# Hybrid encoder layer on one core: all operands of TensorE moved to one start address modulo 256 bytes in SBUF

## The chip, the cores and the metric

The kernel runs on one core of one Trainium2 chip. The metric is the device time of one execution in microseconds. A core has five engines that run side by side: TensorE (PE in the profile: matmuls; PEld: its weight loads, which run beside the matmuls), VectorE (DVE), ScalarE (ACT), GpSimd (POOL) and SyncE (SP, which issues the DMAs). All of them work on SBUF, 128 partitions of a fixed number of bytes each. A tensor in SBUF has a byte address that is the same in every partition; this case is about that address.

## The reference

One layer of a hybrid encoder on 1024 tokens of width 1024, with 16 meta tokens put before them, so 1040 positions, all in float32:

```python
hn = rms_norm(h, g_mix_pre)
proj = hn @ w_in          # c_q 384, c_kv 256, k_rope 64, and seven parts of 1024
a = mla(c_q, c_kv, k_rope, ...)      # 8 heads of attention, softmax over 1040 keys
r = hgrn2(hq, hf_fwd, hf_bwd, hi, hg, lb, g_norm)   # 8 heads, a gated recurrence in both directions
mixed = sigmoid(gate_a) * a + sigmoid(gate_h) * r
h = h + rms_norm(mixed @ w_o, g_mix_post)
hn = rms_norm(h, g_ffn_pre)
ff = (silu(hn @ w_gate) * (hn @ w_up)) @ w_down     # inner width 2816
h = h + rms_norm(ff, g_ffn_post)
```

## The kernel before, in words

Every large product is made in three matmuls. A float32 operand `x` is split in two parts, `x_hi` (rounded to the type float32r) and `x_lo = x - x_hi`, and the helper `three` (lines 81 to 85) adds up `w_hi*x_hi`, `w_hi*x_lo` and `w_lo*x_hi` in one PSUM bank. In a matmul one operand is the weights (128 columns, 512 bytes of each partition, loaded by an instruction of its own while the matmul before is still running) and the other is the moving operand, which streams past them: 512 columns as a rule, 256 to 348 in some places. All three matmuls of `three` therefore name lines 83, 84 and 85 in the profile, whatever the stage. "Triple" below means three such matmuls, and a "block" means the 8 triples (24 matmuls) of one weight block of 128 output channels, k = 0 to 7 over the 1024 input channels.

The stages follow each other in time. In parentheses is where each lies in the profile:

1. `normalize_and_values` (to 140 us): the first norm, and the values of the recurrence. Here the normed tokens (`hn_hi`, `hn_lo`) are the weights, and a quarter of a weight matrix (256 columns) moves. The first 7 of its 36 units run with k outermost: 21 matmuls with one k, then 21 with the next. In all the others k is innermost.
2. `hgrn_heads` (to 932 us): six projections per head and the recurrence. `hn_hi` and `hn_lo` are moving operands here, `[P, 8, 1040]`, one row of 1040 columns for each k. `CHUNKS2` cuts the 1024 tokens in two chunks of 512, `CHUNKS3` the 1040 positions of `ff` in 348, 346 and 346. The list `PE_STEPS` puts the recurrence's own small matmuls (lines 794 to 867, plain float32) at given places between the projections' triples; the lists `ACT_STEPS` and `DVE_STEPS` set the order on the other two engines.
3. `latents` (to 974 us) and `attention_heads` (to 1425 us): for each head, `PIECES` makes the keys (`k_nope`, from `ckv`, in the pieces of `CHUNKS3`) and the queries (from `cq`). Then for each of 8 tiles of 128 queries come the scores against 512, 272 and 256 keys (lines 1512, 1518, 1519; the last 256 are called the tail), the softmax, transposes (line 1551) and the product with the values (moving operands `prob_hi` and `prob_lo`).
4. `output_and_ffn` (to the end): 16 blocks of `w_o`, and for each half of the tokens 22 tiles of gate and up (two blocks each) and the down projection (176 triples). Everything here is 512 columns wide.

Where things lie in SBUF follows from the order in which `sbuf_tensor` is called: a tensor begins where the one before it ends, rounded up to 32 bytes. So a row of 1040 float32 (4160 bytes, 64 more than a multiple of 256) shifts the next row by 64 bytes modulo 256, and a tensor of 1040 columns shifts all tensors behind it. From the addresses in the built program, modulo 256:

| tensor | before | after the change |
|---|---|---|
| `w_hi`, `w_lo` (weights of nearly all stages) | 224 | 128 |
| `hn_hi`, `hn_lo`, row k | 96 + 64 k | 128, all rows |
| `ffn_in` hi, first half of the tokens | 224 | 128 |
| `ffn_in` lo, first half; hi and lo, second half | 96 | 128 |
| `hidden`, `mixed` hi and lo, `cq`, `ckv`, `kr_pair` | 96 | 128 |
| `k_nope` hi / lo of even heads; of odd heads | 224 / 96; 32 / 160 | 128 |
| `q_nope`, `v` (weights) | 224 | 128 |
| `prob_hi`, `prob_lo` | 128 | 128 |
| `vw_hi`, `vw_lo` (move in stage 1) | 96 | 128 |

**Offset** below is the start address of the moving operand minus that of the weights, modulo 256. Before, 1686 of the 9204 float32r matmuls stand at offset 0, 966 at 64, 4498 at 128, 998 at 192, and the rest at 160 or at odd places of chunks of 346.

Of the kernel before, what the change touches and what calls it, by code (L numbers as in the profile page):

```python
# [18 lines left out]
F32 = mybir.dt.float32  # L19
F32R = mybir.dt.float32r  # L20
# [5 lines left out]
P = 128  # L26
# [3 lines left out]
L = SEQ + META  # L30
EPS = 1e-6
# [15 lines left out]
CHUNKS3 = [(0, 348), (348, 346), (694, 346)]  # L47
# [327 lines left out]
def hgrn_heads(nc, t, hn_hi, hn_lo, weights):  # L375
# [9 lines left out]
    with ExitStack() as c:  # L385
# [6 lines left out]
        scan_mask = sb("scan_mask", [P, L], mybir.dt.uint8)  # L392
# [9 lines left out]
        decay = [sb(f"decay{d}", [P, NCH]) for d in (FWD, BWD)]  # L402
# [9 lines left out]
        r = sb("r", [P, HALF])  # L412
        waited = sb("waited", [P, 1])
        bank = [c.enter_context(nc.psum_tensor(f"h_bank{i}", [P, HALF], F32)) for i in range(8)]
# [502 lines left out]

class Latents:

    def __init__(self, t, weights, memory, semaphores):
        def sb(name, shape, dt=F32):
            return memory.enter_context(t.nc.sbuf_tensor(name, shape, dt))

        def signal(name, per):
            return Signal(semaphores.enter_context(t.nc.semaphore(name)), per)

        self.mixed_first = sb("mixed_first", [P, KT, HALF])
        with ExitStack() as place:
            self.mixed_parts = {x: place.enter_context(t.nc.sbuf_tensor(f"mixed_first_{x}", [P, KT, HALF], F32R))  # L930
                                for x in ("hi", "lo")}
        self.parts = {(n, x): sb(f"{n}_{x}", [P, k, w], F32R)
                      for n, k, w in (("cq", QT, SEQ), ("ckv", KVT, LK)) for x in ("hi", "lo")}
        self.kr = sb("kr_pair", [P, L], F32R)
        self.table = sb("rope_table", [P, L])
        self.weights = (*(x[0] for x in weights.blocks()),
                        signal("aw_in", 16), signal("aw_hi_done", 1), signal("aw_lo_done", 1))

def latents(nc, t, lat):  # L940

    with ExitStack() as c:
# [31 lines left out]
        with nc.Block() as block:  # L975
# [27 lines left out]
            def _(act):  # L1003
# [36 lines left out]
                for u in range(len(units)):  # L1040
# [5 lines left out]
                    if u == 6:  # L1046
                        for x, (a, w) in enumerate(CHUNKS3):
                            act.wait_ge(folded, x + 1)
                            act.copy(lat.kr[:, a:a + w], bank[x][:, 0:w]).then_inc(hi_done["kr"], 1)
# [5 lines left out]
            def _(dve):  # L1055
# [15 lines left out]
                for x, (a, w) in enumerate(CHUNKS3):  # L1071
                    dve.wait_ge(hi_done["kr"], x + 1)
                    low = slice(P - ROPE, P)
                    dve.tensor_tensor(lat.kr[low, a:a + w], bank[x][low, 0:w], lat.kr[low, a:a + w].bitcast(F32),
                                      ALU.subtract).then_inc(lo_done["kr"], 1)

            @block.tensor
            def _(pe):
# [8 lines left out]
                for x, (a, w) in enumerate(CHUNKS3):  # L1087
                    pe.matmul(bank[x][:, 0:w], t.const("fold"), turned[:, a:a + w], start=True,
                              stop=True).then_inc(folded, 1)
# [15 lines left out]
def attention_heads(nc, t, weights, lat, used):  # L1105
# [7 lines left out]
    with ExitStack() as c:  # L1113
# [16 lines left out]
        TAIL = HALF // 2  # L1130
        HEAD = L - TAIL
# [6 lines left out]
        top, top_tail, shift = ([sb(f"{n}{i}", [P, QS]) for i in range(2)] for n in ("top", "top_tail", "shift"))  # L1138
        sums, sums_tail, inv = ([sb(f"{n}{i}", [P, QS]) for i in range(2)] for n in ("sums", "sums_tail", "inv"))
        minus_scale = sb("minus_scale", [P, 1])  # L1140
# [3 lines left out]
        rec = [sb(f"rec{i}", [P, HALF]) for i in range(2)]  # L1144

# [9 lines left out]
        PIECES = [("k", 2 * QT, KVT, ckv, a, w, out) for (a, w), out in zip(CHUNKS3, (first, second, tail_bank[:]))]  # L1155
# [40 lines left out]
        with nc.Block() as block:  # L1196
# [72 lines left out]
            def _(act):  # L1269
# [5 lines left out]
                def piece(p, i):  # L1275

                    name, _, _, _, a, w, src = PIECES[i]
                    if name == "k":
# [3 lines left out]
                        act.copy(k_nope["hi", par][:, a:a + w], src[:, 0:w]).then_inc(piece_hi.sem, 1)  # L1282
# [75 lines left out]
            def _(dve):  # L1358
                def piece(p, i):
# [4 lines left out]
                    if name == "k":  # L1364
                        par = p.base % 2
                        dve.tensor_tensor(k_nope["lo", par][:, a:a + w], src[:, 0:w],
                                          k_nope["hi", par][:, a:a + w].bitcast(F32),
# [108 lines left out]
            def _(pe):  # L1476
# [29 lines left out]
                def nope_terms(nxt, j, out, a, w):  # L1506
# [4 lines left out]
                    for n, (q, k) in enumerate((("hi", "hi"), ("hi", "lo"), ("lo", "hi"))):  # L1511
                        pe.matmul(out, q_nope[q, i][:, qs], k_nope[k, par][:, a:a + w], start=(n == 0), stop=False)

                def rope_terms(nxt, j, out, a, w):
# [3 lines left out]
                    pe.matmul(out, q_rope["hi", i][:, qs], kr[:, a:a + w], start=False, stop=False)  # L1518
                    return pe.matmul(out, q_rope["lo", i][:, qs], kr[:, a:a + w], start=False, stop=True)
# [80 lines left out]
def output_and_ffn(nc, t, weights, mixed_first, mixed_out):  # L1600
# [5 lines left out]
    with ExitStack() as c:  # L1606
# [17 lines left out]
        sb("of_raw", [P, 6 * L - KT * HALF - 4 * HALF])  # L1624
# [675 lines left out]
def bass_hybrid_encoder_layer(nc, d, out):  # L2300
    with ExitStack() as ctx:
# [93 lines left out]
```

## Time and profile before

| | |
|---|---|
| median of 3 runs | 2291.48 us (2289.41 to 2291.96) |
| the profiled execution: its time | 2292.32 us |
| its span, first to last instruction | 2290.5 us |
| PE busy | 2199.6 us (96%), 11716 matmuls |
| PEld busy | 1837.8 us (80%), 11716 weight loads |
| DVE / ACT / POOL busy | 47% / 40% / 20% |
| DMA, mean share of 16 engines | about 24% |

The profile gives each instruction a start and a duration. Matmuls overlap: one lasts 0.39 us by the profile, and the next begins 0.23 us after it began. What a matmul costs in a stream is therefore the distance from its start to the start of the next, and that is what is read below. Rows of the timeline give starts to 0.01 us; where a nanosecond is named, it is from the trace's own nanoseconds, and the rows shown are the first and the last of the stretch.

### The profile page before, as it was taken

The page shows a single profiled execution, that of the slowest core. Times are in us where ns is not written, and L with a number is a line of the kernel's source. Part 1 is how long each engine was busy: PE and PEld are TensorE (multiplying, and loading weights), DVE is VectorE, ACT ScalarE, POOL GpSimd, SP SyncE. Part 2 cuts the span into 40 slices and gives each one's busy share as a digit, 9 for nine tenths or more (in the row PEclk, how much of TensorE's full clock was granted, in tenths as well). Part 3 has the DMA queues.
Part 4 walks back from the last instruction along what each step waited for, and adds up shares of the span by engine and source line. Part 5 has one row for each costly group of instructions (what it writes and reads, how often), then busy time and mean ns, then how long its engine had stood idle before and what let it go on. Part 6 is the DMA issues. An engine that isn't in the chain of part 4 may idle for free. (4 is left out here: it accounts for less than half of the span.)

```text
span 2290.5 us, 32058 instructions
## 1 busy us (share of the span) xinstructions
PE 2199.6 (96%) x11716; PEld 1837.8 (80%) x11716; DVE 1083.6 (47%) x1725; ACT 920.2 (40%) x1453; POOL 463.6 (20%) x215
## 2 busy tenths in 40 slices
PE   5999999999999999899999998999999999999997
PEld 4988888888888888678888886768887888878785
DVE  5003664754845746357777776465443002421101
ACT  4223354453543544545455554443333223222222
POOL 3110000000000000111111110134444444444444
PEclk9999999999999999999999998999999999999998
DMA  3221112111121110311111111543432233332233
GB/s 139 73 74 56 42 61 65 36 56 55 46 64 45 56 64 16 117 56 42 43 42 41 41 41 58 171 139 92 132 97 92 93 103 112 115 128 92 92 101 129
DMA packets 76570, 178.42 MB, mean 78 GB/s; under 512 B 6768, under 2 KB 27568, under 8 KB 75984
## 3 DMA queue, kind: packets, MB, share of 16 engines
q1 hardware_dynamic: 76496, 177.41, 24.1%
q8 instruction: 49, 0.80, 0.2%
q14 instruction: 25, 0.20, 0.0%
HBM read 149.99 MB, written 27.39 MB: 77 GB/s over the span
## 5 line engine op out<-in xcount | busy, mean ns | idle before, releaser
L1840 POOL TENSOR_TENSOR w_lo<-w_raw,w_hi 128x1024 fp32r<-128x1024 f32 x136 | 330.8, 2432 | 411.8 <-ACT w_hi L1859 411.8
L83 PE MATMUL h_bank<-hn_hi,w_hi 128*128 128x512 f32 (+2 forms) x952 | 373.5, 392 | 3.9 <-PEq L165 2.5
L84 PE MATMUL h_bank<-hn_lo,w_hi 128*128 128x512 f32 (+2 forms) x952 | 356.3, 374 | 0.0
L85 PE MATMUL h_bank<-hn_hi,w_lo 128*128 128x512 f32 (+2 forms) x952 | 355.8, 374 | 0.0
L83 PE MATMUL f_bank<-ffn_in_hi,w_hi 128*128 128x512 f32 x704 | 279.6, 397 | 1.9 <-POOL w_lo L1840 1.8
L84 PE MATMUL f_bank<-ffn_in_lo,w_hi 128*128 128x512 f32 x704 | 277.4, 394 | 0.0
L85 PE MATMUL f_bank<-ffn_in_hi,w_lo 128*128 128x512 f32 x704 | 277.4, 394 | 0.0
L83 PEld LDWEIGHTS h_bank<-hn_hi,w_hi 128*128 128x128 f32 x952 | 179.1, 188 | 36.7 <-issue 9.9
L85 PEld LDWEIGHTS h_bank<-hn_hi,w_lo 128*128 128x128 f32 x952 | 179.0, 188 | 29.8
L84 PEld LDWEIGHTS h_bank<-hn_lo,w_hi 128*128 128x128 f32 x952 | 179.1, 188 | 28.1 <-issue 3.8
L1859 ACT CAST w_hi<-w_raw 128x1024 fp32r<-128x1024 f32 x136 | 142.2, 1046 | 133.1 <-PE f_bank L85 130.8
L591 ACT COPY raw<-h_bank 128x512 f32<-128x512 f32 (+2 forms) x119 | 63.9, 543 | 283.0 <-PE h_bank L85 253.1
L83 PEld LDWEIGHTS f_bank<-ffn_in_hi,w_hi 128*128 128x128 f32 x704 | 132.4, 188 | 34.8 <-issue 2.1
L993 POOL MEMSET ckv_hi<- 128x224 f32 x1 | 0.3, 285 | 784.8 <-POOLq L463 784.8
L85 PEld LDWEIGHTS f_bank<-ffn_in_hi,w_lo 128*128 128x128 f32 x704 | 132.4, 188 | 31.4
L84 PEld LDWEIGHTS f_bank<-ffn_in_lo,w_hi 128*128 128x128 f32 x704 | 132.5, 188 | 31.2 <-issue 0.7
L83 PE MATMUL f_bank<-hidden_hi,w_hi 128*128 128x512 f32 x352 | 140.4, 399 | 4.9 <-DVE hidden_lo L2019 4.9
L84 PE MATMUL f_bank<-hidden_lo,w_hi 128*128 128x512 f32 x352 | 140.3, 399 | 0.0
L85 PE MATMUL f_bank<-hidden_hi,w_lo 128*128 128x512 f32 x352 | 140.0, 398 | 0.0
L1315 ACT CAST prob_hi<-a_bank 128x512 fp32r<-128x512 f32 x144 | 83.1, 587 | 141.4 <-PE a_bank L1551 141.0
L2028 DVE TENSOR_TENSOR square_sum<-square_sum,f_square 128x512 f32<-128x512 f32 x16 | 11.1, 693 | 241.8 <-ACT f_square L1890 241.8
L770 DVE TENSOR_TENSOR w_lo<-w_raw,w_hi 128x1024 fp32r<-128x1024 f32 x52 | 63.5, 1222 | 109.1 <-ACT w_hi L571 109.1
(339 smaller groups left out, 4422.2 us busy)
## 6 DMA issues: line engine op xcount, KB each, us to landing
w_raw<-in_w_ffn SPq DMA_DIRECT2D x136, 512.0 KB, 3.6
w_raw<-in_w_hgrn SPq DMA_DIRECT2D x54, 512.0 KB, 3.6
w_raw<-in_w_out SPq DMA_DIRECT2D x15, 512.0 KB, 3.6
w_raw<-in_w_head SPq DMA_DIRECT2D x9, 512.0 KB, 5.8
X<-in_x SPq DMA_DIRECT2D x8, 520.0 KB, 6.7
values<-v_stage SPq DMA_DIRECT2D x32, 128.0 KB, 1.7
values_h<-values SPq DMA_DIRECT2D x8, 512.0 KB, 4.8
gate_out<-raw SPq DMA_DIRECT2D x8, 512.0 KB, 2.9
```

Of the source, the lines that this page charges most:

```text
L83: pe.matmul(out, wh, xh, start=start, stop=False)
L84: pe.matmul(out, wh, xl, start=False, stop=False)
L85: return pe.matmul(out, wl, xh, start=False, stop=stop)
L591: act.copy(t.raw[:, s * L + a:s * L + a + w], bank[made.banks[e]][:, 0:w]).then_inc(proj_copied.sem, 1)
L770: dve.tensor_tensor(w_lo[s % 2][:], w_raw[s % 2][:], w_hi[s % 2][:].bitcast(F32), ALU.subtract).then_inc(w_lo_done.sem, 1)
L993: pool.memset(part[:, :, L:].bitcast(F32), 0.0).then_inc(padded, 1)
L1315: act.copy(turned_hi[k % RING][:], turn_bank[k % 2][:]).then_inc(p_hi.sem, 1)
L1840: pool.tensor_tensor(w_lo[i][:], w_raw[i][:], w_hi[i][:].bitcast(F32), ALU.subtract).then_inc(w_lo_done, 1)
L1859: act.copy(w_hi[k % 2][:], w_raw[k % 2][:]).then_inc(w_hi_done, 1)
L2028: dve.tensor_tensor(sq_sum[:], sq_sum[:], square[i][:], ALU.add).then_inc(y_added.sem, 1)
```

## The change

The work is the same, with the same instructions but for some widths. Constants are added for padded sizes, tensors of 1040 columns that hold operands of TensorE are stored with rows of 1088 (`LP`), `raw` is rounded up, a filler `to_row` stands ahead of the weights, and small tensors whose size is no multiple of 256 bytes are allocated behind the large ones. `CHUNKS3` becomes 384, 384 and 272, so that each chunk begins at a multiple of 64 columns. The keys of attention are made in pieces of 384, 400 and 256 (`KEYS`), and the last 256 are stored 48 columns further on (`key_at`), so that the tail too begins at a multiple of 64 columns. After it 9156 float32r matmuls stand at offset 0 and 48 at offset 64 (the pieces of `ckv` at column 784).

```diff
+ROW = 64
+LP = -(-L // ROW) * ROW
+RAW = -(-6 * L // ROW) * ROW
...
-CHUNKS3 = [(0, 348), (348, 346), (694, 346)]
+CHUNKS3 = [(0, 384), (384, 384), (768, 272)]
...
-        cum = [sb("cum_f", [P, L]), sb("cum_b", [P, SEQ])]
-        sub = [sb("sub_f", [P, L]), sb("sub_b", [P, SEQ])]
-        key = [sb("key_f", [P, L]), sb("key_b", [P, SEQ])]
+        cum, sub, key = ([sb(f"{n}_f", [P, LP])[:, 0:L], sb(f"{n}_b", [P, SEQ])[:]] for n in ("cum", "sub", "key"))
...
+TAIL = HALF // 2
+HEAD = L - TAIL
+KEYS = [(0, 384), (384, HEAD - 384), (HEAD, TAIL)]
+
+
+def key_at(a, w):
+
+    a += LP - L if a >= HEAD else 0
+    return slice(a, a + w)
...
-        self.kr = sb("kr_pair", [P, L], F32R)
-        self.table = sb("rope_table", [P, L])
+        self.kr = sb("kr_pair", [P, LP], F32R)
+        self.table = sb("rope_table", [P, LP])[:, 0:L]
...
-        k_nope = {(x, i): sb(f"k_nope_{x}{i}", [P, L], F32R) for x in both_parts for i in range(2)}
+        k_nope = {(x, i): sb(f"k_nope_{x}{i}", [P, LP], F32R) for x in both_parts for i in range(2)}
...
-        PIECES = [("k", 2 * QT, KVT, ckv, a, w, out) for (a, w), out in zip(CHUNKS3, (first, second, tail_bank[:]))]
+        PIECES = [("k", 2 * QT, KVT, ckv, a, w, out) for (a, w), out in zip(KEYS, (first, second, tail_bank[:]))]
...
-                        act.copy(k_nope["hi", par][:, a:a + w], src[:, 0:w]).then_inc(piece_hi.sem, 1)
+                        act.copy(k_nope["hi", par][:, key_at(a, w)], src[:, 0:w]).then_inc(piece_hi.sem, 1)
...
-                        pe.matmul(out, q_nope[q, i][:, qs], k_nope[k, par][:, a:a + w], start=(n == 0), stop=False)
+                        pe.matmul(out, q_nope[q, i][:, qs], k_nope[k, par][:, key_at(a, w)], start=(n == 0), stop=False)
...
-        sb("of_raw", [P, 6 * L - KT * HALF - 4 * HALF])
+        sb("of_raw", [P, RAW - KT * HALF - 4 * HALF])
...
+        ctx.enter_context(nc.sbuf_tensor("to_row", [P, 40], F32))
...
-        with nc.sbuf_tensor("raw", [P, 6 * L], F32) as raw:
+        with nc.sbuf_tensor("raw", [P, RAW], F32) as raw:
...
-            with nc.sbuf_tensor("hn_hi", [P, KT, L], F32R) as hn_hi, nc.sbuf_tensor("hn_lo", [P, KT, L], F32R) as hn_lo:
+            with nc.sbuf_tensor("hn_hi", [P, KT, LP], F32R) as hi, nc.sbuf_tensor("hn_lo", [P, KT, LP], F32R) as lo:
+                hn_hi, hn_lo = hi[:, :, 0:L], lo[:, :, 0:L]
```

On PE nothing changes place, only widths do. The pieces of a head's keys at its start in attention (before; `a_scores` and `a_bank` are PSUM banks, and the number at the end is partitions x columns; the same three rows for the second k are left out in each case):

```order
L83 MATMUL a_scores<-ckv_hi,w_hi 128x348
L84 MATMUL a_scores<-ckv_lo,w_hi 128x348
L85 MATMUL a_scores<-ckv_hi,w_lo 128x348
...
L83 MATMUL a_scores<-ckv_hi,w_hi 128x346
L84 MATMUL a_scores<-ckv_lo,w_hi 128x346
L85 MATMUL a_scores<-ckv_hi,w_lo 128x346
...
L83 MATMUL a_bank<-ckv_hi,w_hi 128x346
L84 MATMUL a_bank<-ckv_lo,w_hi 128x346
L85 MATMUL a_bank<-ckv_hi,w_lo 128x346
```

The same place on PE after the change:

```order
L88 MATMUL a_scores<-ckv_hi,w_hi 128x384
L89 MATMUL a_scores<-ckv_lo,w_hi 128x384
L90 MATMUL a_scores<-ckv_hi,w_lo 128x384
...
L88 MATMUL a_scores<-ckv_hi,w_hi 128x400
L89 MATMUL a_scores<-ckv_lo,w_hi 128x400
L90 MATMUL a_scores<-ckv_hi,w_lo 128x400
...
L88 MATMUL a_bank<-ckv_hi,w_hi 128x256
L89 MATMUL a_bank<-ckv_lo,w_hi 128x256
L90 MATMUL a_bank<-ckv_hi,w_lo 128x256
```

The columns stay 1040 in all; the first two pieces grow and the last shrinks. On ACT the same widths show in the copies of `ff` out of PSUM, in a head of the recurrence. Before:

```order
L591 COPY raw<-h_bank 128x348
L591 COPY raw<-h_bank 128x346
L571 CAST w_hi<-w_raw 128x1024
L531 ACTIVATE decay<-cum_f 128x8
L532 ACTIVATE factor_f<-factor_f 128x1040
L591 COPY raw<-h_bank 128x346
L591 COPY raw<-h_bank 128x512
```

and after, with the copies standing at the same places between the other steps:

```order
L594 COPY raw<-h_bank 128x384 x2
L574 CAST w_hi<-w_raw 128x1024
L534 ACTIVATE decay<-cum_f 128x8
L535 ACTIVATE factor_f<-factor_f 128x1040
L594 COPY raw<-h_bank 128x272
L594 COPY raw<-h_bank 128x512
```

DVE has the same three widths in attention's low parts of the keys and is otherwise unchanged; POOL and SP have the same rows as before.

## Rows read from the trace of the kernel before

**Rows 1.** The page: PE's busy time, and the granted clock in 40 slices.

```profile
PE 2199.6 (96%) x11716; PEld 1837.8 (80%) x11716; DVE 1083.6 (47%) x1725; ACT 920.2 (40%) x1453; POOL 463.6 (20%) x215
...
PEclk9999999999999999999999998999999999999998
```

**Rows 2.** Busy time by stretches: attention, and the feed-forward of the first half.

```profile
974.00:1425.00 451.00, 430.89 (x2434) 368.51 (x2434) 333.13 (x624) 223.92 (x482) 62.13 (x34) 0.98 0.13 42
1524.00:1774.00 250.00, 247.04 (x1060) 198.44 (x1058) 101.05 (x111) 92.36 (x119) 110.80 (x45) 1.00 0.33 103
```

**Rows 3.** Groups by line: count, busy us, mean ns, idle before and its end.

```profile
L83 PE MATMUL h_bank<-hn_hi,w_hi 128*128 128x512 f32 x688 | 287.7, 418 | 1.4 <-ACT raw L591 1.4
L83 PE MATMUL f_bank<-ffn_in_hi,w_hi 128*128 128x512 f32 x704 | 279.6, 397 | 1.9 <-POOL w_lo L1840 1.8
...
L859 PE MATMUL h_bank<-factor_f,state 128*128 128x128 f32 x128 | 24.7, 275 | 0.0
...
L857 PE MATMUL h_bank<-scores,values_h 128*128 128x128 f32 x128 | 24.7, 275 | 0.0
...
L591 ACT COPY raw<-h_bank 128x512 f32<-128x512 f32 (+2 forms) x119 | 63.9, 543 | 283.0 <-PE h_bank L85 253.1
```

**Rows 4.** Timeline of PE, projections: starts of eight whole blocks, first and last.

```profile
158.07 0.40 PE L83 MATMUL h_bank<-hn_hi,w_hi 128*128 128x512 f32 x1
...
159.47 0.39 PE L83 MATMUL h_bank<-hn_hi,w_hi 128*128 128x512 f32 x1
...
160.16 0.40 PE L83 MATMUL h_bank<-hn_hi,w_hi 128*128 128x512 f32 x1
...
202.55 0.40 PE L83 MATMUL h_bank<-hn_hi,w_hi 128*128 128x512 f32 x1
```

**Rows 5.** Timeline of PE, feed-forward: starts at either end of four stretches.

```profile
1530.58 0.40 PE L84 MATMUL f_bank<-ffn_in_lo,w_hi 128*128 128x512 f32 x1
...
1535.62 0.40 PE L85 MATMUL f_bank<-ffn_in_hi,w_lo 128*128 128x512 f32 x1
...
1542.25 0.40 PE L83 MATMUL f_bank<-ffn_in_hi,w_hi 128*128 128x512 f32 x1
...
1636.55 0.40 PE L83 MATMUL f_bank<-ffn_in_hi,w_hi 128*128 128x512 f32 x1
...
1654.10 0.40 PE L83 MATMUL f_bank<-ffn_in_hi,w_hi 128*128 128x512 f32 x1
...
1766.10 0.40 PE L83 MATMUL f_bank<-ffn_in_hi,w_hi 128*128 128x512 f32 x1
...
1916.02 0.39 PE L83 MATMUL f_bank<-ffn_in_hi,w_hi 128*128 128x512 f32 x1
...
2010.82 0.40 PE L83 MATMUL f_bank<-ffn_in_hi,w_hi 128*128 128x512 f32 x1
```

**Rows 6.** Timeline of PE, stage 1: first matmul of k = 2, 3 and 4.

```profile
39.25 0.28 PE L83 MATMUL n_bank<-w_hi,hn_hi 128*128 128x256 f32 x1
...
41.77 0.28 PE L83 MATMUL n_bank<-w_hi,hn_hi 128*128 128x256 f32 x1
...
44.17 0.28 PE L83 MATMUL n_bank<-w_hi,hn_hi 128*128 128x256 f32 x1
```

**Rows 7.** Timeline of PE in attention, an even head: values, then scores.

```profile
1209.14 0.40 PE L84 MATMUL a_bank<-prob_lo,v_hi 128*128 128x512 f32 x1
1209.37 0.40 PE L85 MATMUL a_bank<-prob_hi,v_lo 128*128 128x512 f32 x1
1209.61 0.39 PE L1512 MATMUL a_scores<-k_nope_hi,q_nope_hi 128*128 128x512 f32 x1
...
1210.30 0.28 PE L1512 MATMUL a_scores<-k_nope_hi,q_nope_hi 128*128 128x272 f32 x1
1210.42 0.29 PE L1512 MATMUL a_scores<-k_nope_lo,q_nope_hi 128*128 128x272 f32 x1
...
1211.13 0.29 PE L1518 MATMUL a_scores<-kr_pair,w_hi 128*128 128x272 f32 x1
```

More of the change, by code:

```diff
@@ L401, in hgrn_heads @@
         ends = [factor[d][:, 0:L if d == FWD else SEQ] for d in (FWD, BWD)]
-        decay = [sb(f"decay{d}", [P, NCH]) for d in (FWD, BWD)]
         ends_t = [sb(f"ends_t{d}", [P, NCH, P]) for d in (FWD, BWD)]
@@ L412, in hgrn_heads @@
         r = sb("r", [P, HALF])
+        decay = [sb(f"decay{d}", [P, NCH]) for d in (FWD, BWD)]
         waited = sb("waited", [P, 1])
+        scan_mask = sb("scan_mask", [P, L], mybir.dt.uint8)
         bank = [c.enter_context(nc.psum_tensor(f"h_bank{i}", [P, HALF], F32)) for i in range(8)]
@@ L1046, in _ @@
                     if u == 6:
-                        for x, (a, w) in enumerate(CHUNKS3):
+                        for x, (a, w) in enumerate(KEYS):
                             act.wait_ge(folded, x + 1)
-                            act.copy(lat.kr[:, a:a + w], bank[x][:, 0:w]).then_inc(hi_done["kr"], 1)
+                            act.copy(lat.kr[:, key_at(a, w)], bank[x][:, 0:w]).then_inc(hi_done["kr"], 1)
                     if u == 8:
@@ L1070, in _ @@
                                                  op1=ALU.subtract).then_inc(lo_done[n], 1)
-                for x, (a, w) in enumerate(CHUNKS3):
+                for x, (a, w) in enumerate(KEYS):
                     dve.wait_ge(hi_done["kr"], x + 1)
                     low = slice(P - ROPE, P)
-                    dve.tensor_tensor(lat.kr[low, a:a + w], bank[x][low, 0:w], lat.kr[low, a:a + w].bitcast(F32),
-                                      ALU.subtract).then_inc(lo_done["kr"], 1)
+                    dve.tensor_tensor(lat.kr[low, key_at(a, w)], bank[x][low, 0:w],
+                                      lat.kr[low, key_at(a, w)].bitcast(F32), ALU.subtract).then_inc(lo_done["kr"], 1)
             @block.tensor
@@ L1086, in _ @@
                 pe.wait_ge(turned_done, 1)
-                for x, (a, w) in enumerate(CHUNKS3):
+                for x, (a, w) in enumerate(KEYS):
                     pe.matmul(bank[x][:, 0:w], t.const("fold"), turned[:, a:a + w], start=True,
@@ L1137, in attention_heads @@
         prob = [t.raw[:, 0:QS * L].rearrange("p (j k) -> p j k", j=QS), sb("prob1", [P, QS, L])]
-        top, top_tail, shift = ([sb(f"{n}{i}", [P, QS]) for i in range(2)] for n in ("top", "top_tail", "shift"))
-        sums, sums_tail, inv = ([sb(f"{n}{i}", [P, QS]) for i in range(2)] for n in ("sums", "sums_tail", "inv"))
-        minus_scale = sb("minus_scale", [P, 1])
         RING = 3
@@ L1144, in attention_heads @@
         rec = [sb(f"rec{i}", [P, HALF]) for i in range(2)]
+        top, top_tail, shift = ([sb(f"{n}{i}", [P, QS]) for i in range(2)] for n in ("top", "top_tail", "shift"))
+        sums, sums_tail, inv = ([sb(f"{n}{i}", [P, QS]) for i in range(2)] for n in ("sums", "sums_tail", "inv"))
+        minus_scale = sb("minus_scale", [P, 1])
         def mixed(h, i):
@@ L1365, in piece @@
                         par = p.base % 2
-                        dve.tensor_tensor(k_nope["lo", par][:, a:a + w], src[:, 0:w],
-                                          k_nope["hi", par][:, a:a + w].bitcast(F32),
+                        dve.tensor_tensor(k_nope["lo", par][:, key_at(a, w)], src[:, 0:w],
+                                          k_nope["hi", par][:, key_at(a, w)].bitcast(F32),
                                           ALU.subtract).then_inc(piece_read.sem, 1)
@@ L1517, in rope_terms @@
                     qs = slice(j * P, (j + 1) * P)
-                    pe.matmul(out, q_rope["hi", i][:, qs], kr[:, a:a + w], start=False, stop=False)
-                    return pe.matmul(out, q_rope["lo", i][:, qs], kr[:, a:a + w], start=False, stop=True)
+                    pe.matmul(out, q_rope["hi", i][:, qs], kr[:, key_at(a, w)], start=False, stop=False)
+                    return pe.matmul(out, q_rope["lo", i][:, qs], kr[:, key_at(a, w)], start=False, stop=True)
                 def score_head(nxt, j, p):
```

3 lines of the change are left out of this document (removed).

## The prediction

> **What bounds the kernel now.** I read the page first. PE is busy for 2199.6 us of the 2290.5 us span, and its granted clock stands at 9 or more tenths in nearly every slice [rows 1]: the kernel is a stream of matmuls, and other engines matter only where PE waits for them. The busy times by stretches say where that is: in the feed-forward of the first half PE is busy 247.04 of 250.00 us, in attention 430.89 of 451.00, so 20 us of waits lie there [rows 2]. The groups by line confirm it: the 688 first matmuls of the projections' triples waited 1.4 us in all, those of gate and up 1.9 us [rows 3]. So a nanosecond on each matmul shows in the time nearly in full, except in attention.
>
> The next question is what a matmul costs. In the timeline of the projections eight whole blocks lie between 158.07 and 202.55 us: 44.48 us for 192 matmuls of 512 columns, 5.560 us a block, 231.7 ns each [rows 4]. At the upper level of the clock, 2.4 GHz, 512 columns are 213.3 ns, so 18 ns of each are something else. The change can only reach those 18 ns.
>
> **Does the offset matter at all?** The timeline is very regular, so small differences can be read. I compare stretches whose offset I know from the table of addresses.
>
> - Projections. The offset goes 128, 192, 0, 64 with k. The triple from 159.47 to 160.16 is one at offset 0 [rows 4]. In the trace's nanoseconds the 133 such triples with nothing between them average 691 ns, and the 383 others 697 (128: 697, 192: 697, 64: 696). Offset 0 is thus worth 6 ns a triple. It is never alone for longer than three matmuls here.
> - Scores. Of the 272-column ones, those at offset 0 last 0.28 us and those at offset 128 last 0.29 [rows 7]; start to start that is 121 and 120 ns against 124 to 129. The pair of 512 columns from the product with the values (offset 160) goes at 0.23 and 0.24 us [rows 7], 234 and 235 ns, and the score matmul of 512 columns at offset 0 behind it at 230 ns.
> - Stage 1, 256 columns wide, moving operand at 224. Here runs of 21 matmuls keep one offset. From 39.25 to 41.77 us it is 0: 2.52 us, 120 ns each. From 41.77 to 44.17 it is 192: 2.40 us, 114 ns each, and 113.3 ns once settled [rows 6]. So in the one place where offset 0 lasts, it is the dearest, and 192 the cheapest. This speaks against the change.
> - Feed-forward, all 512 wide, starts at either end of four stretches [rows 5]. 22 matmuls from 1530.58 to 1535.62: 229.1 ns each. 17 blocks from 1542.25 to 1636.55: 5.547 us a block, 231.1 ns. 20 blocks from 1654.10 to 1766.10: 5.600 us, 233.3 ns. These three have the very same operands (two of each three matmuls at offset 0, one at 128) and differ only by what interrupted PE ahead of them. In the second half, all at offset 128, 17 blocks from 1916.02 to 2010.82 take 5.576 us each.
>
> I take from this that a 512-column matmul moves between 226 and 233.3 ns in patterns that lock in and last until PE is interrupted, and that addresses help to choose the pattern without settling it. The float32 matmuls of the recurrence show nothing: 275 ns at offset 192 and at offset 0 alike [rows 3]. They count for nothing.
>
> **The change part by part.**
>
> 1. Projections, 688 triples = 86 blocks of 512 columns, and `ff` and the latents in three chunks, 11 x 1040 columns, about 22 blocks more. All at offset 0, a triple at 0.690 and a block at 5.520 instead of 5.560 us: 108 x 0.040 = **4.3 us** less.
> 2. `w_o` and feed-forward, 1184 triples = 148 blocks. Against 5.520: 20 blocks x 0.027, 24 x 0.080, 44 x 0.056; for the down projection and `w_o`, 60 blocks that I put halfway between the last two stretches, at 5.59, 60 x 0.07. Sum 0.5 + 1.9 + 2.5 + 4.2 = **9.1 us** less.
> 3. Attention. 144 triples with the values from 702 to 690 ns, 1.7 us; 256 of the 320 score matmuls of 272 columns 4 ns less, 1.0; those of 512 columns 0.5; 96 triples of queries 6 ns less, 0.6. Sum 3.8. Some of it only lengthens waits for softmax, as PE has 20 us of idle time there. I take **2.5 us**; both ends, 0 and 3.8, stay in the range.
> 4. 256-column matmuls. Three quarters of the 864 of stage 1 come to offset 0 at 120 ns, from 114 to 119: 2.5 ns each, 1.6 us more; the tails of the scores 0.4. **2.0 us more.**
> 5. Other widths. 384 + 384 + 272 are the same 1040 columns as before, and none of the recurrence's steps on PE lies inside `ff` (the first is at place 36, `ff` ends at 23). 384 + 400 + 256 are 1040 too; ACT's and DVE's copies of them are as long in sum. No instruction and no wait is added. Taken as nothing: ACT waits 253.1 us for PE before those copies [rows 3], so PE's stream hides them. With that cover gone, 36 columns more on a copy of 0.54 us [rows 3] are under 0.05 us, once or twice a head, 1 us in all.
> 6. Addresses of the other engines' operands and of DMAs. They wait for PE in the stretches that count [rows 2, 3], so a few per cent there would not show.
>
> Sum: 4.3 + 9.1 + 2.5 - 2.0 = 13.9 us. The profiled execution took 2292.32 us, of which 1.8 lie outside its span; less 13.9 it is 2278.4. The median of the runs shown is 0.8 under it: **2277 us**, 0.6% faster.
>
> **Rules of the skill beside the rows.** The Trainium skill (TensorE: Matmul & The Clock Gate, "Step-by-step: what each phase is for") says that PE has two independent SBUF read ports, so that the load of the next weights takes nothing from the running matmul's reads. By that rule no offset can matter and the time would stay; rows 6 (2.52 against 2.40 us for the same 21 matmuls) speak against it. The same page ("Back-to-back issue gap") gives N / 2.4 + 2.5 ns, 215.8 ns for 512 columns; no stretch here comes under 226, and if the layout were the whole cause of that, some 256 blocks at 5.18 us would save near 100 us. Nothing in the rows points there: `prob` (aligned to 64 bytes already) goes at 234.
>
> **The rivals.**
>
> - *Offset 0 held all the time locks in the dear pattern*, as it does in stage 1 [rows 6]. Every 512-column matmul then goes at 233.3 ns, a block at 5.600 as from 1654.10 on [rows 5]. Cost: 108 x 0.040 = 4.3, feed-forward 20 x 0.053 + 44 x 0.024 + 60 x 0.01 = 2.7, 256 columns 2.0: 9 us slower, 2300. It decides as soon as the block settles above 5.58. For it: rows 6, and that two of three matmuls at offset 0 did lock at 5.600 once. Against it: the same operands also ran at 229 ns, and short runs at offset 0 are cheap at 272 and 512 columns. 15%.
> - *Offset 0 held all the time reaches the cheap pattern*: twice the settled 113.3 ns of stage 1, 226.7 ns, a block at 5.44. 256 blocks x 0.08 more than forecast, 20 us: 2257. For it: single matmuls of 225 and 226 ns at offset 0. 13%.
> - *The offset is not the cause* (what I read as its effect is the pattern that the interruptions leave). Patterns are dealt anew, gains and losses cancel: within 4 us of 2291. For it: three costs for one set of operands [rows 5]. 12%. By the skill's rule on the two ports this is the case that comes true.
> - *The forecast*, 60%.
>
> **How the numbers follow.** The likeliest case has its own range of 2268 to 2287: a triple at 687 (229 ns, rows 5) instead of 690 takes 6 us more off, one at 693 gives 6 back, attention 2 either way. The whole range goes down to 2255, to hold most of the cheap pattern, and up to 2293, which leaves out the dear one and a little of no change. A run of this kernel tells 0.2%, 4.6 us, from no change. Faster: 0.60 + 0.13; same 0.12; slower 0.15.
>
> **What would show it.** In the profile after: blocks of the projections at 5.52 us, the same in both halves of the feed-forward; stage 1's runs all at 2.52 us; scores of 272 columns at 0.28 us in even and odd heads alike; `PEclk` and the idle times as before. Blocks at 5.60, or blocks that still differ from stretch to stretch at one and the same offset, would prove me wrong on the cause, and blocks at 5.44 on the size.

## The result

| | before | after |
|---|---|---|
| median | 2291.72 us (2289.41 to 2292.90, 4 runs) | 2265.76 us (2265.05 to 2266.65, 4 runs) |
| the profiled execution: its time, its span | 2292.32, 2290.5 us | 2265.73, 2263.9 us |
| mean granted clock | 0.990 | 0.989 |

The ratio is 0.9888, with an interval of 0.9871 to 0.9905: 26 us or 1.1% faster, where the forecast said 0.6%, 14.5 us under the median of the three runs shown (its own sum is 13.9 us). The direction and the range held. The size did not: the time lies below the likeliest case's own range (2268 to 2287), between the forecast and the rival "reaches the cheap pattern" (2257).

The page after, PE's busy time and the granted clock, to be set beside [rows 1]:

```profile
PE 2172.3 (96%) x11716; PEld 1838.8 (81%) x11716; DVE 1082.2 (48%) x1725; ACT 920.4 (41%) x1453; POOL 463.0 (20%) x215
...
PEclk9999999999999999999999999999999999999998
```

PE has lost 27.3 us of busy time, and the span 26.6. What PE does not fill was 90.9 us and is 91.6, and the clock is the same. Waits are as long as before: each matmul costs less. The groups of [rows 3] have these counterparts, with the same counts, and the idle time ahead of them has grown by less than a microsecond:

```profile
L88 PE MATMUL h_bank<-hn_hi,w_hi 128*128 128x512 f32 x688 | 285.6, 415 | 1.6 <-ACT raw L594 1.6
...
L88 PE MATMUL f_bank<-ffn_in_hi,w_hi 128*128 128x512 f32 x704 | 275.5, 391 | 2.6 <-POOL w_lo L1853 2.6
```

Busy time by stretches of the kernel after: the projections with the recurrence, attention, and the feed-forward (gate and up) of the first and the second half. Columns: stretch, length, then PE, PEld, DVE, ACT and POOL busy with their counts, granted clock, DMA share, GB/s.

```profile
142.10:926.30 784.20, 776.56 (x4713) 663.83 (x4713) 448.61 (x782) 344.94 (x500) 2.11 (x6) 1.00 0.17 52
967.80:1417.20 449.40, 429.08 (x2433) 368.55 (x2433) 332.27 (x624) 223.92 (x482) 62.32 (x36) 0.98 0.13 42
1515.10:1760.20 245.10, 241.88 (x1061) 198.83 (x1061) 101.47 (x112) 92.54 (x119) 110.36 (x45) 1.00 0.34 105
1881.60:2126.30 244.70, 240.75 (x1059) 198.19 (x1058) 72.06 (x84) 75.67 (x96) 105.36 (x44) 1.00 0.36 114
```

The stretches begin and end at the first matmul of a stage. From the same starts in both traces comes the table by stage, in us; the last row runs to the end of the kernel, with some 14 us behind the last matmul:

| stage | before | after | difference | forecast |
|---|---|---|---|---|
| 1: norm and values | 123.5 | 124.6 | +1.1 | +1.6 |
| 2: projections, recurrence | 788.9 | 784.2 | -4.7 | term 1, with the latents: -4.3 |
| 3: latents | 43.7 | 41.5 | -2.2 | |
| 3: attention | 451.0 | 449.4 | -1.6 | -2.5, and +0.4 for the tails |
| 4: `w_o` | 98.9 | 98.0 | -1.0 | term 2: -9.1 in all |
| 4: gate and up, both halves | 500.9 | 489.8 | -11.1 | |
| 4: down, both halves | 266.1 | 259.0 | -7.1 | |

The last three give 19.2 us where term 2 had 9.1. The reason stands in the timeline. Two stretches of 20 blocks, one in each half of the feed-forward, first and last start (start, duration, engine, line, operation):

```profile
1638.69 0.39 PE L88 MATMUL f_bank<-ffn_in_hi,w_hi 128*128 128x512 f32 x1
...
1747.54 0.39 PE L88 MATMUL f_bank<-ffn_in_hi,w_hi 128*128 128x512 f32 x1
...
2004.49 0.39 PE L88 MATMUL f_bank<-ffn_in_hi,w_hi 128*128 128x512 f32 x1
...
2113.31 0.39 PE L88 MATMUL f_bank<-ffn_in_hi,w_hi 128*128 128x512 f32 x1
```

108.85 and 108.82 us for 20 blocks: 5.442 us each, 226.8 ns a matmul, in both halves alike. Before, it was 5.547 and 5.600 in the first and 5.576 in the second [rows 5]. In the trace's nanoseconds 667 of the 701 whole triples of gate and up are 680 ns exactly. The forecast had 690. In the projections the longest stream, eight blocks of it:

```profile
158.49 0.39 PE L88 MATMUL h_bank<-hn_hi,w_hi 128*128 128x512 f32 x1
...
202.01 0.39 PE L88 MATMUL h_bank<-hn_hi,w_hi 128*128 128x512 f32 x1
```

43.52 us, 5.440 a block, against 5.560 in [rows 4]. But such a stream is rare in the projections. What the recurrence's small matmuls leave behind looks like this:

```profile
256.92 0.45 PE L845 MATMUL h_bank<-factor_b 128*32 128x32 f32 x16
257.29 0.50 PE L88 MATMUL h_bank<-hn_hi,w_hi 128*128 128x512 f32 x1
257.63 0.39 PE L89 MATMUL h_bank<-hn_lo,w_hi 128*128 128x512 f32 x1
257.86 0.40 PE L90 MATMUL h_bank<-hn_hi,w_lo 128*128 128x512 f32 x1
258.09 0.39 PE L88 MATMUL h_bank<-hn_hi,w_hi 128*128 128x512 f32 x1
258.32 0.40 PE L89 MATMUL h_bank<-hn_lo,w_hi 128*128 128x512 f32 x1
258.56 0.39 PE L90 MATMUL h_bank<-hn_hi,w_lo 128*128 128x512 f32 x1
258.79 0.39 PE L88 MATMUL h_bank<-hn_hi,w_hi 128*128 128x512 f32 x1
```

The distances are 0.34, 0.23, 0.23, 0.23, 0.24 and 0.23 us; in nanoseconds 335, 230, 236, 229, 232, 231, and only then 227, 226, 227 for as long as the stream lasts. The 512-column matmuls of this stage stand in 148 unbroken runs (a run is here a row of matmuls with none of another kind between them), 64 of them of only 3 or 6. By place in the run the mean distance is:

| place after the first | 1 | 2 | 3 | 4 | 5 | 6 | 7 | 8 | 9 | 14 and on |
|---|---|---|---|---|---|---|---|---|---|---|
| before, ns | 232.2 | 232.4 | 231.0 | 231.6 | 232.5 | 231.2 | 233.1 | 232.2 | 231.2 | 231.7 |
| after, ns | 231.9 | 233.6 | 228.3 | 229.5 | 230.3 | 227.3 | 228.3 | 227.8 | 226.7 | 226.7 |

So the cheap pattern is not there at once. Here it takes three to nine matmuls of one offset to reach it, and a shorter run gains little.

Stage 1 is as forecast. The starts of k = 2, 3 and 4 in [rows 6] have these counterparts:

```profile
39.34 0.28 PE L88 MATMUL n_bank<-w_hi,hn_hi 128*128 128x256 f32 x1
...
41.86 0.28 PE L88 MATMUL n_bank<-w_hi,hn_hi 128*128 128x256 f32 x1
...
44.38 0.28 PE L88 MATMUL n_bank<-w_hi,hn_hi 128*128 128x256 f32 x1
```

2.52 us both times, 120 ns a matmul. Attention, for [rows 7] (all heads stand at offset 0 now), first the product with the values:

```profile
1155.68 0.48 PE L88 MATMUL a_bank<-prob_hi,v_hi 128*128 128x512 f32 x1
1155.99 0.40 PE L89 MATMUL a_bank<-prob_lo,v_hi 128*128 128x512 f32 x1
1156.23 0.40 PE L90 MATMUL a_bank<-prob_hi,v_lo 128*128 128x512 f32 x1
1156.46 0.28 PE L1525 MATMUL a_bank<-k_nope_hi,q_nope_hi 128*128 128x256 f32 x1
```

and just ahead of it the scores of 272 columns:

```profile
1153.99 0.40 PE L1525 MATMUL a_scores<-k_nope_hi,q_nope_lo 128*128 128x512 f32 x1
1154.23 0.29 PE L1525 MATMUL a_scores<-k_nope_hi,q_nope_hi 128*128 128x272 f32 x1
1154.35 0.29 PE L1525 MATMUL a_scores<-k_nope_lo,q_nope_hi 128*128 128x272 f32 x1
1154.48 0.29 PE L1525 MATMUL a_scores<-k_nope_hi,q_nope_lo 128*128 128x272 f32 x1
1154.61 0.40 PE L1531 MATMUL a_scores<-kr_pair,w_hi 128*128 128x512 f32 x1
```

The values' pair goes at 0.24 and 0.23 us as before, and the scores of 272 columns last 0.29 and stand 0.12 to 0.13 apart. The sentence that they would all last 0.28 was wrong.

### The profile page after: what moved, and what is told of

It reads as the page before. It is cut to its first block and busy times, and to the rows that moved or that the text cites. A ratio compares the mean times of both kernels' runs of the same rounds, so it can differ in the third digit from the quotient of the medians.

```text
span 2263.9 us, 32058 instructions
## 1 busy us (share of the span) xinstructions
PE 2172.3 (96%) x11716; PEld 1838.8 (81%) x11716; DVE 1082.2 (48%) x1725; ACT 920.4 (41%) x1453; POOL 463.0 (20%) x215
## 5 line engine op out<-in xcount | busy, mean ns | idle before, releaser
L2041 DVE TENSOR_TENSOR square_sum<-square_sum,f_square 128x512 f32<-128x512 f32 x16 | 11.1, 692 | 235.4 <-ACT f_square L1903 235.4
```

The lines of the kernel that those rows point to most:

```text
L2041: dve.tensor_tensor(sq_sum[:], sq_sum[:], square[i][:], ALU.add).then_inc(y_added.sem, 1)
```

## The experiments

All of them start from the kernel after the change, and all but the two on the widths change only where tensors lie in SBUF; the work is the same in every one. Ratios are against the kernel before, which gave medians of 2291.5 to 2292.1 us beside them. The offsets named are those of nearly all wide matmuls; the product with the values and the scores against `k_nope`, whose weights lie behind the fillers too, stay at 0.

### Alignment or difference

Everything 32 bytes further, weights and moving operands alike, so that all start at 160 modulo 256 and the offset stays 0:

```diff
-        ctx.enter_context(nc.sbuf_tensor("to_row", [P, 40], F32))
+        ctx.enter_context(nc.sbuf_tensor("to_row", [P, 48], F32))
```

> The changed kernel with the filler ahead of the weights 8 columns (32 bytes) longer: every operand of TensorE begins at 160 modulo 256 in place of 128, and offset 0 is kept. Theory A (what counts is the offset between moving operand and weights): blocks stay at 5.440 us, time 2266 us. Rival B (what counts is that operands begin at multiples of 64 bytes, which they did nowhere before, at 32 modulo 64): blocks go back to 5.56 to 5.60 us, time about 2290 us.

2265.23 us (2263.62 to 2267.41), ratio 0.988 (0.9864 to 0.9897). Twenty blocks of gate and up:

```profile
1641.38 0.39 PE L88 MATMUL f_bank<-ffn_in_hi,w_hi 128*128 128x512 f32 x1
...
1750.30 0.39 PE L88 MATMUL f_bank<-ffn_in_hi,w_hi 128*128 128x512 f32 x1
```

108.92 us, 5.446 a block. Starts at multiples of 64 bytes are not what counts: the difference of the two addresses is, and rival B, alignment, falls.

### The offset as a dose

A filler behind the weights, 16, 32 or 48 columns wide, sets one offset for nearly all wide matmuls: 64, 128 or 192.

```diff
         ctx.enter_context(nc.sbuf_tensor("to_row", [P, 40], F32))
...
+        ctx.enter_context(nc.sbuf_tensor("shift", [P, 16], F32))
```

> The changed kernel with a filler of 64 bytes between the weights and all that lies behind them: projections, latents' users, w_o and feed-forward stand at offset 64 throughout, stage 1 (whose weights are the tokens) at 192, scores and values in attention stay at 0. Theory A (the offset decides): blocks of 512 columns near the 696 ns a triple that offset 64 had before, 5.57 us, so about 2295 us less 5 us in stage 1, where runs of 21 go from 2.52 to 2.38 us: about 2290 us. Rival B (multiples of 64 bytes decide) and rival C (any offset will do as long as it never changes): blocks stay at 5.440 us, time 2266 or less.

> The same with a filler of 128 bytes: offset 128 in projections, w_o and feed-forward, 128 in stage 1, 0 in scores and values. Theory A: blocks at 5.576 or 5.600 us, as the second half of the feed-forward had them before at offset 128, 256 blocks x 0.15 = 38 us over the changed kernel, about 2300 us. Rivals B and C: blocks at 5.440 us, 2266 us.

> The same with a filler of 192 bytes: offset 192 in projections, w_o and feed-forward, 64 in stage 1, 0 in scores and values. Theory A has two forms. A1 (short runs tell: offset 192 had 695 to 697 ns a triple before): blocks at 5.57 us, about 2295 us. A2 (long runs tell: in stage 1 offset 192 settled at 113.3 ns for 256 columns, 16 cycles over the columns, where offset 0 settled at 120.0, 32 over): 512 columns at 220.0 ns, blocks at 5.28 us, 256 blocks x 0.16 = 41 us less than the changed kernel, about 2225 us. Rivals B and C: 2266 us.

Offset 64: ratio 0.9922 (0.9901 to 0.9944). Its four executions took 2271.20, 2271.64, 2277.11 and 5471.96 us; the ratio leaves out the last, for which no trace is kept, and the median of the other three is 2271.64 us (2274.37 with it). Offset 128: 2291.52 us, 0.9998 (0.9988 to 1.0009). Offset 192: 2295.15 us, 1.0015 (1.0005 to 1.0024). Twenty blocks in the first half of the feed-forward, at offset 64:

```profile
1641.00 0.39 PE L88 MATMUL f_bank<-ffn_in_hi,w_hi 128*128 128x512 f32 x1
...
1750.86 0.39 PE L88 MATMUL f_bank<-ffn_in_hi,w_hi 128*128 128x512 f32 x1
```

at offset 128:

```profile
1650.69 0.39 PE L88 MATMUL f_bank<-ffn_in_hi,w_hi 128*128 128x512 f32 x1
...
1762.69 0.39 PE L88 MATMUL f_bank<-ffn_in_hi,w_hi 128*128 128x512 f32 x1
```

and at offset 192:

```profile
1648.51 0.40 PE L88 MATMUL f_bank<-ffn_in_hi,w_hi 128*128 128x512 f32 x1
...
1760.51 0.40 PE L88 MATMUL f_bank<-ffn_in_hi,w_hi 128*128 128x512 f32 x1
```

109.86, 112.00 and 112.00 us: 5.493, 5.600 and 5.600 us a block. Offset 128 has both of the patterns that the kernel before had at this offset: the other three long stretches of its gate and up go at 5.577. So one offset can still hold two patterns there. Offset 192 is not the mirror of 64 (triples of 700 against 687 ns); the form of the theory in which only the distance around the circle of 256 bytes counts falls. The whole gain of the change, and a little more, is undone by a filler of 192 bytes.

Offset 64 shows two patterns within one unbroken stretch, in the down projection of the first half:

```profile
1765.05 0.40 PE L88 MATMUL f_bank<-hidden_hi,w_hi 128*128 128x512 f32 x1
...
1793.05 0.40 PE L88 MATMUL f_bank<-hidden_hi,w_hi 128*128 128x512 f32 x1
...
1798.57 0.39 PE L88 MATMUL f_bank<-hidden_hi,w_hi 128*128 128x512 f32 x1
...
1864.53 0.39 PE L88 MATMUL f_bank<-hidden_hi,w_hi 128*128 128x512 f32 x1
```

Five blocks in 28.00 us, 5.600 each, and then twelve in 65.96 us, 5.497 each. The change comes with no pause and no other matmul between them; what brought it about is not known. A pattern need not last until PE is interrupted, and a stream can stay in the dear one for more than a hundred matmuls at an offset that has a cheaper one.

Rival C, that any offset will do as long as it never changes, falls with offsets 128 and 192, and form A2, which took the price from 256 columns, with 192. Two of the expectations missed: offset 64 was put at 2290 us from its price in the mixed cycle before (696 ns a triple) and took some 19 us less, and offset 128 was put at 2300, because every block was counted as if it lay in a long stretch.

In the trace's nanoseconds the settled streams differ in kind too. At offset 0 every distance is 226 or 227. At 64 they go round 232, 226 and 229, and at 192 they alternate between 236 and 231. A single distance therefore does not give the price of its offset.

### Between the steps

Fillers of 8 and 56 columns, offsets 32 and 224:

> The changed kernel with a filler of 32 bytes between the weights and what lies behind them: offset 32 in projections, w_o and feed-forward, 224 in stage 1. If the cost rises evenly with the offset (0: 680.0 ns a triple, 64: 686.7, 128: 697, 192: 700 so far), a triple is near 683 ns and the time near 2269 us. If the SBUF is cut in pieces of 64 bytes and only the piece counts, it is 680 or 687 exactly: 2266 or 2274 us.

> The same with 224 bytes: offset 224 in projections, w_o and feed-forward. If the cost jumps between 192 (700) and 256 = 0 (680), 224 is on one side of the jump: a triple at 700, 2295 us, or, if stage 1's settled 113.3 ns at offset 192 means that the best offset is just under 0, less than 680: 2260 us or below. If it falls evenly, 690 ns: 2280 us.

2294.54 us, ratio 1.0003 (0.9994 to 1.0013), and 2294.77 us, ratio 1.0011 (1.0002 to 1.0021). Offset 32:

```profile
1652.22 0.40 PE L88 MATMUL f_bank<-ffn_in_hi,w_hi 128*128 128x512 f32 x1
...
1764.22 0.40 PE L88 MATMUL f_bank<-ffn_in_hi,w_hi 128*128 128x512 f32 x1
```

112.00 us, 5.600 a block, triples at 700.0 ns; offset 224 the same. That is a surprise, and the expectation of 2266 to 2274 us missed: 32 bytes off, the cost is not between those of 0 (680) and 64 (687) but the dearest of all. At 224 the first of the three cases expected, 700 ns and 2295 us, came true. Neither an even rise with the distance nor a cost by pieces of 64 bytes fits. The triple of 512 columns at one constant offset:

| offset, bytes | 0 | 32 | 64 | 128 | 192 | 224 |
|---|---|---|---|---|---|---|
| triple, ns | 680 | 700 | 687, at times 700 | 697 to 700 | 700 | 700 |
| block, us | 5.44 | 5.60 | 5.49, five of 5.60 | 5.58 and 5.60 | 5.60 | 5.60 |

### One offset, or offset 0?

Only `w_lo` is moved, 192 bytes on. The first two matmuls of a triple stay at offset 0, the third comes to 64:

```diff
-        self.raw, self.hi, self.lo = (sb(f"w_{n}", [P, 2 * KT * P], dt)
-                                      for n, dt in (("raw", F32), ("hi", F32R), ("lo", F32R)))
+        self.raw, self.hi = (sb(f"w_{n}", [P, 2 * KT * P], dt) for n, dt in (("raw", F32), ("hi", F32R)))
+        sb("shift_lo", [P, 48], F32)
+        self.lo = sb("w_lo", [P, 2 * KT * P], F32R)
+        sb("shift_back", [P, 16], F32)
```

> The changed kernel with w_lo alone moved by 192 bytes and the rest brought back, so that two of three matmuls keep offset 0 to w_hi and the third operand's weights (w_lo) stand at offset 64 to the moving operand. In each triple the load of w_lo runs beside the second matmul (w_hi with x_lo). Form N of theory A (the stream collides with the load of the next weights): the second matmul of a settled triple grows, the third stays at 226.7 ns. Form O (a matmul's own weights count): the third grows. In both forms a triple lies between 680 and 687 ns, about 682, and the time near 2270 us. If mixing offsets is what costs (the first half of the feed-forward before had two at 0 and one at 128, and took 693 to 700), a triple is over 687 and the time above 2275 us.

2286.40 us (2281.34 to 2289.51), ratio 0.9971 (0.9958 to 0.9984). Twenty blocks:

```profile
1651.04 0.40 PE L88 MATMUL f_bank<-ffn_in_hi,w_hi 128*128 128x512 f32 x1
...
1761.97 0.40 PE L88 MATMUL f_bank<-ffn_in_hi,w_hi 128*128 128x512 f32 x1
```

110.93 us, 5.547 a block, a mean triple of 693 ns. Offset 0 alone gives 680 and offset 64 alone 687; a mixture of the two is dearer than either. The kernel before, with two matmuls at offset 0 and one at 128, had the same 5.547 in one stretch, and 5.600 in another [rows 5]. So two things count: which offset, and that it stays the same. The run was also meant to tell whether a matmul collides with its own weights' address (form O) or with the load that runs beside it (form N). Neither form came out as it was put. In the trace's nanoseconds the settled stream repeats every twelve matmuls: 224, 232, 226, then 227, 226, 236, then 228, 233, 241, then 238, 231, 231. By place in the triple that is 229, 230.5 and 233.5 on average. All three are above 226.7, the third the most, where form N had left the third at 226.7 and both forms had a triple of about 682. Which load matters stays open.

### The widths

Only `CHUNKS3` back to 348, 346 and 346, whose second and third chunk then begin off a multiple of 64 columns:

```diff
-CHUNKS3 = [(0, 384), (384, 384), (768, 272)]
+CHUNKS3 = [(0, 348), (348, 346), (694, 346)]
```

> The changed kernel with only CHUNKS3 put back to 348, 346 and 346, so that ff and the latents' projections start at odd offsets while everything else stays. Theory A: 11 groups of 1040 columns go back from about 11.3 to about 11.45 us, 1.7 us, time 2267 to 2268 us; the widening of the chunks was a small part of the change. Rival D (the chunks matter more, since each odd start leaves PE in a dear pattern for the 512-column blocks behind it): 5 us or more, 2271 us or above.

2265.12 us (2262.88 to 2267.50), ratio 0.9874 (0.9856 to 0.9892). No loss, and not the 1.7 us that was expected. And the layout alone, with the old chunks, the old pieces of the keys, and no gap of 48 columns ahead of the tail:

```diff
-KEYS = [(0, 384), (384, HEAD - 384), (HEAD, TAIL)]
+KEYS = CHUNKS3
...
-    a += LP - L if a >= HEAD else 0
```

> The changed kernel with all its widths and places of keys put back: chunks of 348, 346 and 346 for projections and keys, no gap of 48 columns before the last 256 keys; only the fillers, the padded rows and the order of allocation stay. Projections of 512 columns, w_o, feed-forward and scores of 512 and 272 columns keep offset 0, the 256-column tails of the scores go to 64. If the offset alone matters, and offset 64 costs 256 columns no more than 0 does: 2266 us, within 2 us of the changed kernel. Rival D (the cut of the keys matters): 3 us or more apart.

2268.15 us (2266.08 to 2270.53), ratio 0.9898 (0.9882 to 0.9915), whose interval overlaps that of the full change. By the medians widths, pieces and gap together are worth 2.4 us of the 26, which the intervals do not tell from nothing; the rest comes from the padding. Rival D, that the cut of the keys is worth 3 us or more, finds no support, though an interval this wide does not rule it out. Attention takes 451.3 us in this trace, as before the change, against 449.4 after it; but unchanged stages wander by as much, as the next run shows.

### Only the rows of the projections

`hn_hi` and `hn_lo` back to rows of 1040 columns, everything else as after the change. The offset then cycles with k again in stage 2:

```diff
-            with nc.sbuf_tensor("hn_hi", [P, KT, LP], F32R) as hi, nc.sbuf_tensor("hn_lo", [P, KT, LP], F32R) as lo:
+            with nc.sbuf_tensor("hn_hi", [P, KT, L], F32R) as hi, nc.sbuf_tensor("hn_lo", [P, KT, L], F32R) as lo:
```

> The changed kernel with the rows of hn_hi and hn_lo back at 1040 columns: the offset in projections goes 0, 64, 128, 192 with k again, everything else stays at offset 0. Projections lose what they had gained (788.9 us before, 784.2 after) and attention and feed-forward keep theirs: 2266 + 5 to 6 = about 2271 us. If a pattern once lost in the projections carried over to later stages, or if their mixed offsets were not what cost, it is 2280 or 2266 us.

2271.03 us (2265.69 to 2271.92), ratio 0.9911 (0.9894 to 0.9927). The stretch of stage 2:

```profile
140.40:929.70 789.30, 783.24 (x4713) 663.98 (x4713) 448.54 (x782) 344.65 (x500) 2.14 (x6) 1.00 0.16 51
```

789.3 us against 784.2 after the change: +5.1. The blocks are back at 5.560, and the triple at offset 0 in this cycle is at 692 ns, while the same operands at the same offset, held all the time, take 680. In the profiled execution, the fastest of the four, other stages were shorter by as much in sum, and its time, 2265.69 us, is that of the full change. Stage 1 is 1.4 us shorter for a reason: the rows of `hn_hi` and `hn_lo` are its weights, so its offset cycles with k too, and its matmuls take 118.4 ns in place of 120.0, as they had before the change. That everything else stays at offset 0, as the expectation had it, is not so. Attention is 1.6, `w_o` 1.5 and the latents 1.1 us shorter with nothing changed in them, which is how far such stages can wander between two programs. The median shows 5.3 us more than after the change, but the two intervals overlap; that the rows cost 5 us rests on the stretch and its blocks.

### The narrow operands

In the kernel before 256 columns had been cheapest at offset 192 [rows 6]. The run with the filler of 16 columns (offset 64 elsewhere) confirmed it: there the normed tokens, stage 1's weights, lie 64 bytes further and its `w` part stands at 192, and takes 113.6 ns on average. So `vw`, half of stage 1's moving operands, is put there, with everything else as after the change:

```diff
+        sb("shift_vw", [P, 48])
...
+        sb("shift_back", [P, 16])
```

> The changed kernel with the second weight buffer of stage 1 (vw) 64 bytes lower, so that the 432 matmuls of its parts 1 and 3 stand at offset 192, the cheap one in runs of 256 columns (113.3 ns against 120.0 at offset 0). 432 x 6.7 ns = 2.9 us: about 2263 us, if PE is what bounds those parts; if ACT's copies of the results or the DMAs bound them, no change from 2266.

2263.74 us (2262.37 to 2264.45), ratio 0.9875 (0.9859 to 0.9892), the best that was measured, though its interval overlaps with that of the change. The stretch in which only `vw` moves, after the change:

```profile
61.50:87.50 26.00, 25.93 (x216) 25.96 (x217) 0.00 (x0) 6.63 (x15) 4.62 (x1) 1.00 0.22 73
```

and here:

```profile
61.70:86.30 24.60, 24.57 (x217) 24.60 (x218) 0.00 (x0) 6.59 (x15) 4.61 (x1) 1.00 0.23 77
```

216 matmuls in 26.00 us, 120 ns each, against 217 in 24.60, 113.4 each. Stage 1 takes 121.8 us instead of 124.6. PEld is busy without a gap in both, where in the feed-forward it is busy 198.83 of 245.10 us. A load lasts 188 ns by the profile, at 256 columns as at 512, so that loads overlap one another where one starts every 113 or 120 ns. Whether this is why the best offset is another at this width is not shown.

## Why the prediction was right, and where it was not

- **That the offset matters, and that one offset everywhere is cheaper.** Right, and shown: fillers of 32 to 224 bytes behind the weights, with no other change, move the time from 2266 to between 2272 and 2295 us. The rival "the offset is not the cause" falls. The Trainium skill (TensorE: Matmul & The Clock Gate, "Step-by-step: what each phase is for") says that loading the next weights takes no read bandwidth from the running matmul, and the prediction had weighed that no offset could matter by this rule. The measurement decides against that for this kernel: the difference of the two start addresses costs up to 6.6 ns a matmul (226.7 against 233.3). Whether this happens at the ports or behind them, no run here shows.
- **Term 1, the triple at 0.690.** This is the step that was mis-sized, here and in term 2, and the sign that the prediction had named for a wrong size, blocks at 5.44 us, is what came. The 0.690 was read from single triples at offset 0 between others at 128, 192 and 64 (691 ns). The run with rows of 1040 shows that this is a price of the mixture: the same triple takes 692 ns in the cycle and 680 when the offset is held. The term was 4.3 us and came out at 6.9 with the latents. Had the block of 5.44 held everywhere it would have been 108 x 0.12 = 13 us; the short runs between the recurrence's steps took the rest. In the trace the 512-column matmuls of stage 2 give 500.9 us before and 495.7 after, and those of `ff` 132.0 and 132.5: the three chunks gained nothing. The recurrence's own part, what is left of the stage, is about 156 us both times, as the prediction had it.
- **Term 2, 9.1 us.** Right mechanism, mis-sized by the same 0.080 us a block: 148 x 0.080 = 11.8 more than forecast, 10.1 measured. The stretches are long here, so nearly all blocks settle. Both halves are alike, as the prediction said they would be.
- **Term 3, 2.5 us.** 1.6, which is no more than this stage wanders between programs without a change in it. The distances say more. The values' matmuls went from 234.0 to 230.6 ns and the queries from 232.9 to 227.6 on average, 2.4 us in all; the scores gave nothing (512 columns: about 232 both times) or lost (272 columns: a median of 125 ns, where single ones at offset 0 had been at 121). Five matmuls between two others never reach the settled pattern.
- **Term 4, 2.0 us more.** Right for stage 1 (120 ns; those at other offsets had averaged 117.8, and the stage grew by 1.1 us); the tails of the scores did not rise (118 ns).
- **Terms 5 and 6, nothing.** Right as far as the runs can tell: `CHUNKS3` put back gives the same time, all widths put back 2.4 us more within overlapping intervals, and DVE, ACT and POOL are busy for as long as before.
- **The rival "locks in the dear pattern"** was wrong for offset 0 but describes offsets 32, 192 and 224: a block of 5.600, and 2295 us where it had said 2300. Its main evidence came from 256 columns, where offset 0 is the dearest and 192 the cheapest, and that does not carry over to 512.
- **The rival "reaches the cheap pattern"** had the right block, 5.44, and was too large by 9 us because it let every matmul reach it. The time lies nearer to this rival, given 13%, than to the forecast, and outside the range of the likeliest case. The cause was argued beforehand and the runs bear it out; that the time fell into the whole range is owed to its having been stretched to 2255 for this rival.
- **The patterns** were said to lock in and last until PE is interrupted. The run at offset 64 changes from 5.600 to 5.49 us a block in the middle of a stretch, so the second half of that does not hold in general.
- **The argument on the widths**, that under 512 columns a weight load is over at half time: the trace does not bear it out. By the profile a load lasts 188 ns of the 227 or 233 there, and 188 ns under 256 columns too.

What I would weigh differently: single matmuls of 225 and 226 ns, and twice the settled 113.3 of stage 1, were known and pointed to 226.7; the average over a mixed cycle had been trusted more than they. The match with the doubled 113.3 is in part chance, though: it was taken at offset 192, where 512 columns settle at 233.3.

Still open: what in the hardware makes offset 0 cheap and 32 dear for 512 columns, why 256 columns want 192, and with which load a matmul's reads collide. The runs give the costs, not the mechanism.

## What to carry to other kernels

When TensorE is the bound, read the distance from start to start in a long undisturbed stream. At the upper level of the clock the best here, for float32r and 384 columns or more, was the columns plus 32 cycles; if a stream stays above that, look at where moving operands and weights start modulo 256 bytes, and pad rows (1040 to 1088 floats) so that all stand at offset 0 and none changes from matmul to matmul. For 256 columns 192 was the better offset. Do not read the price of an offset from single instructions in a mixed stream, measure a kernel in which it is held, and count on a gain only where more than some nine matmuls follow each other. A filler tensor of some bytes is a cheap experiment: between the best and the dearest one here lie 30 us, 1.3%.

## What was not expected of the hardware

- The settled distance at offset 0 is 120.0 ns for 256 columns, 173.3 for 384, 180.0 for 400 and 226.7 for 512. At 2.4 GHz that is the columns and 32 cycles each time. 272 columns do not settle on one distance even in the 24 of a row in `ff`: 121 to 130 ns, 125 on average. The dear pattern of 512 columns, 233.3 ns, is 48 cycles.
- 32 bytes between the starts cost as much as 192 or 224 (triple 700 ns), while 64, once settled, cost only 7 ns more than 0.
- A mixture of offsets 0 and 64 within a triple (693 ns) is dearer than either alone (680 and 687).
- 256 columns go at 113.4 ns at offset 192 and at 120.0 at offset 0; 512 columns at 233.3 and 226.7.
- After an interruption the stream goes through one of a few sequences before it settles (335, 230, 236, 229, 232, 231 or 314, 232, 231 ns are the most common), which come back to within a nanosecond or two.
